# Up products of 36 expert blocks moved ahead of the choice and spread of the experts, in a three-layer transformer kernel on one core

## What is computed

```python
q = (xt @ w_q).reshape(T, PEER_HEADS, PEER_QDIM)
s1 = einsum('thd,hkd->thk', q[..., :half], keys1)
s2 = einsum('thd,hkd->thk', q[..., half:], keys2)
v1, i1 = top_k(s1, 16);  v2, i2 = top_k(s2, 16)
cand = v1[..., :, None] + v2[..., None, :]
sv, pos = top_k(cand, 16)
eidx = take(i1 * 128 + i2, pos);  gw = softmax(sv)
y = sum over the chosen experts e: gelu(x . u_tab[e]) * gw[e] * v_tab[e]
```

## Time and profile before

| | us |
|---|---|
| median of 3 runs | 3386.98 (3381.04 to 3396.82) |
| profiled execution, device time | 3379.55 |
| its span | 3377.8 |

### The profile page before, as it was taken

The page is one execution under the profiler, slowest core; times in us unless marked ns, Lnnn a source line. Parts: engine busy times, 40 slices in busy tenths (PEclk is TensorE's granted clock), DMA queues, the critical chain, the costliest instruction groups (busy, mean ns, idle before and its releaser), DMA issues.

```text
span 3377.8 us, 53195 instructions
## 1 busy us (share of the span) xinstructions
PE 3076.7 (91%) x19008; PEld 2712.4 (80%) x19008; DVE 2061.3 (61%) x3619; ACT 1342.0 (40%) x1953; POOL 20.9 (1%) x41
## 2 busy tenths in 40 slices
PE   8997699998999999999999898798926899999999
PEld 8986476898998798988898668784725799999998
DVE  5563543656557556567555636863599766666666
ACT  4332422444443434443444323331318644444443
POOL 0000000000000000000000000000000000000000
PEclk9999899999999999999999868898968999999999
DMA  7556143555554655554555314233410355555554
GB/s 246 186 161 188 56 162 119 174 184 201 184 183 131 219 185 186 184 172 143 198 184 189 124 54 140 90 100 113 155 44 0 101 187 186 187 187 188 187 187 157
DMA packets 141255, 525.50 MB, mean 156 GB/s; under 512 B 16154, under 2 KB 16154, under 8 KB 138320
## 3 DMA queue, kind: packets, MB, share of 16 engines
q1 hardware_dynamic: 134768, 490.79, 44.4%
q0 software_dynamic: 5520, 30.97, 2.8%
q10 hardware_dynamic: 848, 2.10, 0.2%
HBM read 520.65 MB, written 3.15 MB: 155 GB/s over the span
## 4 chain that ended last, share of the span: by engine, by line
PE 81%; DVE 12%; ACT 3%; DMA 2%; issue 2%; ACTq 0%; SPq 0%; DVEq 0%
PE psum L487 74%; PE psum L1464 2%; DMA ring<-wstream 2%; DVE wpair L458 1%; ACT small L1835 1%; DVE arena L2340 1%; PE psum L1033 1%; PE psum L611 1%; PE psum L1056 1%; ACT hpair L1839 1%; PE psum L1045 1%; PE psum L1449 0%; DVE xpair L666 0%; DVE arena L2540 0%; DVE arena L2454 0%
## 5 line engine op out<-in xcount | busy, mean ns | idle before, releaser
L487 PEld LDWEIGHTS psum<-xpair,wpair 128*128 128x128 f32 x11712 | 1461.7, 194 | 78.0 <-DVE wpair L458 41.0
L487 PE MATMUL psum<-xpair,wpair 128*128 128x256 f32 x11712 | 1475.5, 286 | 50.4 <-DVE wpair L458 38.2
L458 DVE TENSOR_TENSOR wpair<-ring,wpair 128x1024 fp32r<-128x1024 f32 (+1 forms) x872 | 1060.5, 1220 | 664.9 <-ACT wpair L455 662.6
L455 ACT CAST wpair<-ring 128x1024 fp32r<-128x1024 f32 (+1 forms) x872 | 908.1, 1044 | 1045.8 <-PE psum L487 913.9
L487 PE MATMUL psum<-wpair,hpair 128*128 128x512 f32 x3120 | 757.1, 391 | 3.4 <-DVE hpair L819 3.2
L487 PEld LDWEIGHTS psum<-wpair,hpair 128*128 128x128 f32 x3120 | 569.2, 188 | 113.8 <-issue 6.0
L487 PE MATMUL psum<-wpair,xpair 128*128 128x512 f32 (+3 forms) x1536 | 353.0, 391 | 15.6 <-DVE wpair L458 12.2
L487 PEld LDWEIGHTS psum<-wpair,xpair 128*128 128x128 f32 x1536 | 290.0, 195 | 76.9 <-DVE wpair L458 9.8
L796 ACT ACTIVATE small<-psum 128x256 f32<-128x256 f32 x260 | 99.9, 384 | 456.6 <-PE psum L487 456.6
L815 DVE TENSOR_TENSOR small<-small,arena 128x256 f32<-128x256 f32 x128 | 81.4, 636 | 141.6 <-ACT small L796 141.6
L611 PE MATMUL psum<-kc,arena 128*128 128x128 f32 (+1 forms) x212 | 44.2, 374 | 122.2 <-DVEq L2550 67.3
(11 more groups left out here) (305 smaller groups left out, 1617.1 us busy)
## 6 DMA issues: line engine op xcount, KB each, us to landing
ring<-wstream SPq DMA_DIRECT2D x934, 512.0 KB, 3.4
arena<-rows POOLq DMA_DIRECT2D x18, 1024.0 KB, 5.7
arena<-diag POOLq DMA_DIRECT2D x2, 1728.0 KB, 10.3
tbuf<-arena POOLq DMA_DIRECT2D x1, 2048.0 KB, 44.7
arena<-tbuf POOLq DMA_DIRECT2D x2, 1024.0 KB, 9.4
arena<-x_feat ACTq DMA_DIRECT2D x4, 256.0 KB, 8.7
res<-x_tok ACTq DMA_DIRECT2D x1, 1024.0 KB, 10.9
arena<-mem_feat POOLq DMA_DIRECT2D x1, 1024.0 KB, 5.0
```

Of the source, the lines that this page charges most:

```text
L455: eng.copy(hi, raw).then_inc(S("w_hi"), 1)
L458: eng.tensor_tensor(wpair[:, 1, o % PAIRS, 0:w], raw, hi.bitcast(F32), ALU.subtract)\
L487: mm = pe.matmul(out_, a[i], b[j], start=start and n == 0, stop=stop_ and last)
```

## The change

The order of the 256 slots of the expert blocks changes, and with it the order of the work. The first 24 up products stand between the last scores and the transposes; their GELU goes to a buffer `ga` of its own, their low weight halves are made by GpSimd. Twelve more are put one after every fifth group of the spread, their GELU goes to `gb`. The spread no longer copies the weights of the first 24 blocks into `wexp`: VectorE multiplies them from PSUM onto `ga`, and ScalarE copies the other 104 columns when that is done. The blocks left then run in 36 rounds of one up and two downs, and after those in rounds of one up and one down. In a round ScalarE does the GELU and then the weight casts. In the choice, the values `v16` are copied to PSUM, and the rank tables lie there. VectorE makes two low halves fewer before the choice. The scratch for DMA descriptors is set to 4096. The spread's loops are written out.

```diff
+NA, NB = 24, 12
+N0 = NA + NB
+def peer_up(f):
+    return f if f <= N0 else N0 + 1 + 3 * (f - N0 - 1) if f <= 2 * N0 else 4 * N0 + 1 + 2 * (f - 2 * N0 - 1)
+def peer_down(f):
+    if f < N0:
+        return N0 + 1 + 3 * f + 2
+    if f < 2 * N0:
+        return N0 + 1 + 3 * (f - N0) + 1
+    return 2 * NKEY - 1 if f == NKEY - 1 else 4 * N0 + 1 + 2 * (f - 2 * N0) + 1
...
+        gb = sb("gb", [P, NB, SEQ])
...
+            def round3(k, i=0):
+                pe_peer_up(pe, N0 + 1 + k, i, 4)
+                pe_peer_down(pe, 2 * k, N0 + k, i, 8)
+                pe_peer_down(pe, 2 * k + 1, k, i, 8)
+            def round2(f, i=0):
+                pe_peer_up(pe, f + 1, i, 6)
+                pe_peer_down(pe, f, f, i, 6)
...
+            def early_tile(k, i, wi):
+                h = 2 * k + 1
...
+                if k < NA:
+                    src = ga[:, bass.ds(k + 4 * i, 1), :].rearrange("p o s -> p (o s)")
                 else:
+                    src = whole(h)
+                    g = gb[:, bass.ds(k - NA + 4 * i, 1), :].rearrange("p o s -> p (o s)")
+                    dve.tensor_tensor(src, g, weight(k + 4 * i), ALU.mult).then_inc(S("hid_whole"), 1)
...
+                dve_halves(dve, h, src, H0 + h + 1 + 8 * i)
+            def round3(k, i=0):
...
+                for j in range(2):
+                    split.one(o + N0 + 4 + 3 * k + j, i)
+                fresh_tile(k + 1, 2 * k + 2, i, wi, 8, 4)
+                early_tile(k + 1, i, wi)
+                split.one(o + N0 + 6 + 3 * k, i)
...
-        caf = region(23040, NT, 8, 16)
-        cbf = region(23296, NT, 8, 16)
+        v16p = psum[:, 0, :].rearrange("p (t c k) -> p t c k", t=NT, c=16)
+        caf = psum[:, 1, 0:256].rearrange("p (t h k) -> p t h k", t=NT, h=8)
+        cbf = psum[:, 1, 256:512].rearrange("p (t h k) -> p t h k", t=NT, h=8)
+        cbt3 = region(23296, NT, 8, 16)
...
+            split.at = ORDER[STAGES["peer"].slot][1]
+            pool.wait_ge(S("w_lo"), split.at)
+            split.to(split.at + NA + 2)
...
             scores(4)
+            for f in range(NA):
+                pe_peer_up(pe, f)
             pe.wait_ge(S("selected"), 1)
...
+            for n in range(SEQ // 4):
+                pe.wait_ge(S("oh_ready"), n + 1)
+                pe.wait_ge(S("oh_act"), n + 1)
...
                 mm.then_inc(S("w_done"), 1)
+                if n % 5 == 4 and n // 5 < NB:
+                    pe_peer_up(pe, NA + n // 5)
             pe.wait_ge(S("w_out"), SEQ // 4)
-            pe_ffn(pe, "peer", peer=True)
+            pe_peer(pe)
...
+            split.to(o + 3)
+            for f in range(NA):
+                early(f)
+                split.to(o + min(f + 4, NA + 2))
+                if f == 17:
+                    act.wait_ge(S("top_shift"), 1)
...
+            for n in range(SEQ // 4):
+                act.wait_ge(S("w_mul"), n + 1)
+                act.copy(wexp[:, 4 * n:4 * n + 4, :], psum[:, n % 4, :].rearrange("p (s e) -> p s e", s=4)[:, :, NA:])\
+                   .then_inc(S("w_out"), 1)
+                if n + 2 < SEQ // 4:
+                    onehot(n + 2)
+                if n % 5 == 1 and n > 5:
+                    early(NA + n // 5 - 1)
+                if n % 5 == 2 and n // 5 < NB:
+                    split.to(o + NA + 3 + n // 5)
...
-                    split.cover("pq", n)
+                    split.cover("pq", n, more=2 if n < 3 else 0)
...
+            chain(copy(v16p.rearrange("p t c k -> p (t c k)"), v16[:, :, :, :].rearrange("p t c k -> p (t c k)")))
...
+            for n in range(SEQ // 4):
+                g = ga[:, :, 4 * n:4 * n + 4]
+                dve.wait_ge(S("w_done"), n + 1)
+                dve.tensor_tensor(g, g, psum[:, n % 4, :].rearrange("p (s e) -> p e s", s=4)[:, 0:NA, :], ALU.mult)\
+                   .then_inc(S("w_mul"), 1)
+                if n + 2 < SEQ // 4:
+                    onehots(n + 2)
+                if n % 5 == 3 and n // 5 < NB:
+                    split.to(o + NA + 3 + n // 5)
...
-    nc = bacc.Bacc("TRN2", target_bir_lowering=False, num_devices=1)
+    nc = bacc.Bacc("TRN2", target_bir_lowering=False, num_devices=1, dynamic_dma_scratch_size=4096)
```

More of the change, by code:

```diff
@@ L711, in up @@
                                  [xpair[:, a, k, :] for a in (0, 1)], k == 0, k == KD - 1,
[L712 removed]
+                                 "hid_done" if j == 1 and k == KD - 1 else None)
                     hold(slot)
             def down(f, i=0):
[L716 removed]
+                slot = s.slot + down_slot(f)
                 w = weights(pe, slot, i)
@@ L726, in down @@
                 hold(slot)
[L728 to L742, removed]
+            body, head = LOOP // 3, 2
             turns = (n - head - 1) // body
@@ L755, in pe_ffn, with pe_last_downs @@
                     down(f)
-            last_downs()
+            pe_last_downs(pe, s, f0 + n - 2, [s.slot + down_slot(n - 2), s.slot + down_slot(n - 1)])
+        def pe_last_downs(pe, s, h, slots):
+            ws_ = []
+            for t, nn, j in ((0, 0, 0), (0, 1, 0), (0, 0, 1), (0, 1, 1), (1, 0, 0), (1, 0, 1), (1, 1, 0), (1, 1, 1)):
+                if (t, nn) == (0, 0):
+                    ws_.append(weights(pe, slots[j]))
+                    pe.wait_ge(S("hid_out"), h + j + 1)
+                products(pe, bank(s.tile + nn, t), [hpair[:, a, (h + j) % 2, tt(t)] for a in (0, 1)],
+                         part(ws_[j], slice(nn * HALF, (nn + 1) * HALF)), False, j == 1,
+                         f"lin_done{t}" if j == 1 else None)
+            for slot in slots:
+                hold(slot)
@@ new lines, in build, with pe_peer_up @@
+        H0 = FT0["peer"]
+        D0 = H0 - 2 * (H0 // NF)
+        def pe_peer_up(pe, f, i=0, step=0):
+            s = STAGES["peer"]
+            pe.wait_ge(S("hid_act"), H0 + f - 1 + step * i)
+            slot = s.slot + peer_up(f)
+            w = weights(pe, slot, i)
+            for k in range(KD):
+                x_part(pe, k)
+                products(pe, psum[:, 4 + f % 2, 0:SEQ], part(w, slice(k * P, (k + 1) * P)),
+                         [xpair[:, a, k, :] for a in (0, 1)], k == 0, k == KD - 1,
+                         "hid_done" if k == KD - 1 else None)
+            hold(slot)
@@ new lines, in pe_peer_down @@
+        def pe_peer_down(pe, h, f, i=0, step=0):
+            s = STAGES["peer"]
+            slot = s.slot + peer_down(f)
+            w = weights(pe, slot, i)
+            pe.wait_ge(S("hid_out"), H0 + h + 1 + step * i)
+            for nn in range(2):
+                for t in range(NT):
+                    products(pe, bank(s.tile + nn, t), [hpair[:, a, h % 2, tt(t)] for a in (0, 1)],
+                             part(w, slice(nn * HALF, (nn + 1) * HALF)), h == 0, False,
+                             "down_done" if nn + t == 2 else None)
+            hold(slot)
@@ L818, in step @@
[L818 to L822, removed]
+                h = f0 + f
+                dve.tensor_tensor(whole(h), gated(h), psum[:, 4 + h % 2, SEQ:2 * SEQ], ALU.mult)\
+                   .then_inc(S("hid_whole"), 1)
+                dve.wait_ge(S("hid_whole"), h + 1 + i)
```

262 lines of the change are left out of this document (169 added, 93 removed).

## The result

The changed kernel takes 3332.76 us in the median of 4 runs (3330.96 to 3338.63), beside 3384.01 of the kernel before (4 runs, 3377.38 to 3396.82): a ratio of 0.9847, with a 95% interval of 0.9814 to 0.988. So it is faster by 1.5%. The forecast was 3331, in a range of 3304 to 3362. The profiled execution is the one of 3330.96 us; its span is 3329.2 us, 48.6 less than the 3377.8 of before, where 55.7 less was forecast. The total came out nearly right, and two of its three terms not: they missed in opposite directions, so that the near hit of the total is in part luck.

A forecast was written before the change was run, and what follows sets the result against it. TensorE bounds the last stage, but waits for VectorE in the selection and ScalarE in the spread. Span 3377.8 + 9.4 + 36.6 - 101.7 = 3322.1 us, 55.7 less; from the 3386.98 median, 3331, range 3304 to 3362.

The forecast's parts named there:

- The bound: Last stage: TensorE never waits, so work moved out shortens it one for one; 36 ups of 2.88 us, 103.7 us off.
- The last stage: The expert blocks: 103.7 us off for 36 ups, 2.0 us more at the first down, sum -101.7, leaving 624.6 us.
- Can the helpers follow?: Rounds of up, down, down: TensorE needs 8.36 us, ScalarE 3.5 and VectorE 6.4, so both keep up.
- if the rounds are longer than TensorE's work: Last stage: a named sign that the forecast is wrong; rounds of 8.36 us were expected.
- The selection: Choice of experts beside 24 early ups: transposes come 9.4 us later, bounds -0.6 and +30.
- The port: Selection: GpSimd assumed to collide with VectorE's casts and two-input instructions all in SBUF, not those with a PSUM operand; 11 us.
- half an instruction for each of 11: Selection: VectorE's wait for GpSimd at 11 instructions that come while it works, 11 x 1.2 x (2.4/2.88) = 11 us.
- the 13: Selection: VectorE's 13 casts and like or two-input instructions with all operands in SBUF; from above each waits 2.4 us, 31 us.
- Rival (a): Selection: VectorE loses 31 us to GpSimd, or low halves take near 3.9 us; 20 us worse, 3351; 16%.
- The spread: One-hot stage with 12 ups: 140.8 us against 104.6, +36.6 with the last copy; bounds +22 and +57.
- the hand-worked scheme: Spread: five groups and one up take 3 x 1.75 + 5.9 = 11.15 us, VectorE waiting during the up.
- About nothing: Gain of the 12 ups in the spread: they take 34.6 us from the end and give 36.6 back.

The follow-up runs named there:

- experiment 1: Changed kernel with the next up's weight cast ahead of the GELU in rounds of one up and one down: 3330.44 us, ratio 0.9829.
- experiment 6: Changed kernel with cast first, quarter ups, two (second kernel: three) spread ups before the transposes, and both ends of the last stage reordered: 3299.65 us (three: 3302.26).
- experiment 2: Changed kernel with the copied values and the rank tables back in SBUF instead of PSUM: 3367.59 us in one execution.
- experiment 3: Changed kernel with the 12 ups of the spread put in one row behind its last group: 3340.26 us in one execution.
- the version with three more early ups: Changed kernel with cast first, quarter ups, reordered last-stage ends and three of the 12 spread ups ahead of the transposes: 3302.26 us, ratio 0.9741.
- experiment 4: Changed kernel with each of the 12 spread ups split into four parts of 6 matmuls, one after each of four groups: 3317.24 us, ratio 0.9803.
- the version with two more: Changed kernel with cast first, quarter ups, reordered last-stage ends and two of the 12 spread ups ahead of the transposes: 3299.65 us, ratio 0.9737.

## Why the prediction was right or wrong

- **The bound.** Right. Work moved out of the last stage shortens it one for one when the helpers follow: 36 rounds of 8.34 us replace 72 of 5.62, 36 x (2 x 5.62 - 8.34) = 104.4 us, where 103.7 was forecast.
- **The last stage.** Forecast 624.6, measured 639.2. The step that failed is one that wasn't worked out. "Can the helpers follow?" was asked of the new rounds of three alone, and these ran at 8.34 us as forecast. The rounds of one up and one down were taken over at their old 5.62 us. But their GELU is put ahead of both casts as well, which ties the next up to the end of the one before. Each costs 0.21 us more, 54 of them 11.4, shown by experiment 1. VectorE and ScalarE were both far from full in the sums; a chain isn't seen in a sum of busy time. The prediction had named this sign of being wrong, "if the rounds are longer than TensorE's work", and for these rounds it came true. The first down waits 2.44 us, 2.18 more than in the earlier trace rows, as forecast (2.0). The last downs wait 2.73 us; before they waited 0.63. The prediction has no term for that end: 2.1 us of the same order of GELU and cast, and 1.65 more because the 18 matmuls behind the longer wait took 5.97 us at a granted clock of 0.72 instead of 4.32 at 1.00 (experiment 6). The rounds of three gave 0.7 more than forecast. 11.4 + 0.2 + 2.1 + 1.65 - 0.7 = 14.65: that is the whole miss.
- **The selection.** Forecast 9.4 later, measured 10.4. Of that 2.4 us came from ahead of the change: the last low half of the query weights is made at 2469.2 instead of 2466.7 by the same work. So the stage's own part is 8.0, and the contention was put at 11. Added up over the lines, VectorE's instructions that stretch do so by 8.4 us, of which the rows below show two. With the 0.69 us copy, less 2.36 for the two low halves, and 1.2 us in gaps it comes to about 8. Here too a term too large and one too small nearly cancelled.
- **The port.** Right in kind: the casts, copies and SBUF products stretch (one copy of 128 columns took 2312 ns instead of 224), and the compares with a PSUM operand stay at 415 ns in the median and 426 at most. The inputs decide it: the product at 2524.35 below writes to PSUM, reads SBUF twice and is held. That it would be half an instruction for each of 11 was a guess that came near in sum, and a lucky one: some of the 13 weren't touched at all, and one lost 2.09 us. Rival (a) would have been the case with the tables in SBUF, experiment 2. GpSimd's 2.4 us, taken at twice VectorE's row, was measured at 2.409.
- **The spread.** Forecast 36.6, measured 28.1. The multiply was put at 0.3 us a group and VectorE's turn at 1.75. One takes 250 ns, but starts overlap, so that the turn is 1.60 us (experiment 3), 0.15 more than the 1.45 of before. Put into the hand-worked scheme, 1.60 gives 3 x 1.60 + 5.7 = 10.5 for five groups, and 10.33 was measured. So the scheme held within 0.2 us and the multiply was the mis-sized term. "About nothing" for the 12 ups was right: 4.4 us. Its 36.6 mixed two things, though: 64 x (1.75 - 1.634) = 7.4 us were the multiply's, which measured -2.1, and the 29.2 left were the ups', which measured 30.2.
- **The sum.** 1.0 us too little for the selection, 8.5 too much for the spread and 14.6 too little for the last stage: 7.1 us in all, so the span fell by 48.6 and not by 55.7. The medians differ by 51.3 us; the kernel before took 3384.01 beside it, 3.0 less than the median that I had started from, so that the time itself came out 1.8 from the forecast. The range held.

Two instructions of the choice that stretch, in VectorE's timeline of the kernel after; the cast of 512 columns is the 0.43 us row:

```profile
2495.57 1.91 DVE L2684 CAST arena<-arena 128x512 f32<-128x512 uint32 x1
...
2524.35 1.93 DVE L2729 TENSOR_TENSOR psum<-arena 128x256 f32<-128x256 f32 x1
```

And the spread from 2565 to 2680 in groups by line: ScalarE's copy and VectorE's multiply (busy, mean ns, idle ahead):

```profile
L2049 ACT COPY arena<-psum 128x416 f32<-128x416 f32 x55 | 27.6, 502 | 14.3 <-DVE arena L2775 14.3
...
L2775 DVE TENSOR_TENSOR arena<-arena,psum 128x96 f32<-128x96 f32 x55 | 13.8, 250 | 13.5 <-PE psum L1800 13.5
```

ScalarE's copy shrank from 576 ns to 502, as forecast.

## What to carry to other kernels

When an order within a round is changed, walk the chain of one round (who must end before whom, start to start), also for those rounds that keep their length: the busy sums left both helpers a third of the time or more, and the chain was 0.2 to 0.3 us longer than the one product that covered it. Look at the two ends of a stage as well: a wait there can cost TensorE's clock on top. A product put into a stage that another engine paces should be cut to pieces shorter than that stage's slack: the same 24 matmuls cost 2.5 us in one piece and 1.24 in four. Give GpSimd work beside VectorE where VectorE reads PSUM, and look at each of VectorE's instructions for its operands first.

## What the runs showed of the hardware

Not everything beside GpSimd is either held or free. The big reductions of the choice read one tensor, 4096 elements in a strided order, and took 7.00 us each in the kernel before, where GpSimd was idle. Both of them in the kernel after, where GpSimd works for most of the first and for 1.2 us of the second:

```profile
2531.74 7.70 DVE L2739 TENSOR_REDUCE arena<-arena 128x256 f32<-128x4096 f32 x1
...
2544.90 7.04 DVE L2739 TENSOR_REDUCE arena<-arena 128x256 f32<-128x4096 f32 x1
```

In the version with three more early ups, where GpSimd works beside both, they take 7.69 and 7.70 us. They are slowed by about 10%, but not stopped, beside GpSimd; why, no run here shows. The Trainium skill (SBUF — State Buffer, Who interferes with whom) counts such a reduction among what is never touched; here it is, and the measurement decides.

A wait of the same length doesn't always cost the clock. The first downs of the last stage waited 2.44 us in the kernel after and in experiments 3 and 4. Their 24 matmuls took 5.71 us at a granted clock of 1.00 in the first, and 7.31 and 7.30 us at 0.77 in the other two. So experiment 4's last stage is 640.8 us, 1.6 longer than the 639.2 of the kernel after, for the same work.

The stages ahead of the change are not at the same place in every run. The work is the same, yet the first early up began at 2475.84 in the kernel after, 2490.11 in experiment 1, 2494.58 in experiment 2, 2468.59 in experiment 4 and 2478.96 in the version with two more: 26 us, more than every single effect tested. The granted clock, as the mean of the execution, goes the other way: 0.947 in experiment 2, 0.951 in experiment 1, 0.955 in the kernel after and 0.959 in experiment 4. The window from 380 to 400 us shows such a difference, in the kernels before and after, whose work is the same there (columns as above):

```profile
380.00:400.00 20.00, 16.38 (x75) 13.02 (x75) 9.70 (x25) 8.66 (x33) 0.00 (x0) 0.69 0.00 1
```

```profile
380.00:400.00 20.00, 18.98 (x72) 16.10 (x71) 8.57 (x22) 7.20 (x28) 0.00 (x0) 0.50 0.00 0
```

In the same 20 us TensorE had a granted clock of 0.69 in one execution and of 0.50, its lower level of 1.2 GHz, in the other, and did 72 matmuls instead of 75. So an effect of 10 us was read from its own stage and not from the total. Left open is which of VectorE's instructions a lock will catch in the choice: that depends on what arrives first, and no run fixed this order.
